# Three stage starts, two mask tables, one tail and one attention's copies put elsewhere in the queues of a fused two-model kernel

## What is computed

```python
def reference(x, mem, positions, ...):
    x = first_block(x, mem, positions, ...)
    return second_block(x, ...)

# first_block, layer i of 2
x = x + dsa_moba_mixer(h, ...)            # i = 0: top-64 keys for 8 heads, block attention for 8 heads
x = x + nsa_mixer(h, ...)                 # i = 1
x = x + memory_cross_attention(rms_norm(x), rms_norm(mem), ...)
x = x + swiglu(rms_norm(x), ffn_w_in, ffn_w_out)

# second_block, layer l of 2
proj = rmsnorm(x) @ w_in                  # gates 4096, conv 512, three attentions 2048
ys = conformer conv, neighbourhood, dilated and sliding-window attention (4 heads each)
mixed = sum(sigmoid(gate_n + b_n) * (ys_n @ w_branch_n))
x = x + mixed @ w_out
x = x + (silu(gate) * up) @ w_down        # gate, up = split(conv3(rmsnorm(x) @ w_up))
```

## Time and profile before

| | us |
|---|---|
| median of 3 runs | 1684.88 (1684.46 to 1686.14) |
| profiled execution, its own time | 1684.49 |
| its span, first to last instruction | 1682.7 |
| PE busy in it | 1626.0 (97%) |
| DVE busy | 1096.4 (65%) |
| ACT busy | 885.1 (53%) |
| POOL busy | 456.2 (27%) |

### The profile page before, as it was taken

How to read it: one execution, slowest core, us unless ns; L and a number is a source line. 1 busy time by engine, 2 the same in 40 slices (tenths; PEclk the granted TensorE clock), 3 DMA queues, 4 the chain that set the end, 5 groups by cost and what they waited for, 6 DMA issues and landing times. The chain is left out here.

```text
span 1682.7 us, 26946 instructions
## 1 busy us (share of the span) xinstructions
PE 1626.0 (97%) x10929; PEld 1465.7 (87%) x10929; DVE 1096.4 (65%) x1546; ACT 885.1 (53%) x1385; POOL 456.2 (27%) x476
## 2 busy tenths in 40 slices
PE   8989899999999999999999999999999999999999
PEld 7857799987887879998888998999888899889997
DVE  6875656545576765655577668677646866867773
ACT  7454554434455555443446746566445674665652
POOL 2500200002341120000237805144213790504430
PEclk9999999999999999999999999999999999999999
DMA  7522466556340236665554434766556444376652
GB/s 275 171 75 91 110 181 195 178 199 207 103 150 26 76 101 169 187 193 185 177 191 151 151 126 131 197 182 192 180 160 211 155 150 129 127 197 178 189 187 75
DMA packets 287068, 265.30 MB, mean 158 GB/s; under 512 B 12257, under 2 KB 247521, under 8 KB 286945
## 3 DMA queue, kind: packets, MB, share of 16 engines
q1 hardware_dynamic: 286944, 263.59, 50.4%
HBM read 262.52 MB, written 1.05 MB: 157 GB/s over the span
## 5 line engine op out<-in xcount | busy, mean ns | idle before, releaser
L144 DVE TENSOR_TENSOR w_lo<-w_raw,w_hi 128x2048 fp32r<-128x2048 f32 (+2 forms) x244 | 568.8, 2334 | 296.7 <-ACT w_hi L143 294.5
L1863 PE MATMUL bank<-h_hi,w_hi 128*128 128x256 f32 x1984 | 566.2, 285 | 11.9 <-issue 4.6
L143 ACT ACTIVATE w_hi<-w_raw 128x2048 fp32r<-128x2048 f32 (+2 forms) x244 | 462.4, 1901 | 207.4 <-PE bank L529 117.4
L1864 PE MATMUL bank<-h_lo,w_hi 128*128 128x256 f32 x1984 | 561.9, 283 | 0.0
L1865 PE MATMUL bank<-h_hi,w_lo 128*128 128x256 f32 x1984 | 561.9, 283 | 0.0
L1863 PEld LDWEIGHTS bank<-h_hi,w_hi 128*128 128x128 f32 x1984 | 380.8, 192 | 16.4 <-issue 10.9
L1864 PEld LDWEIGHTS bank<-h_lo,w_hi 128*128 128x128 f32 x1984 | 381.0, 192 | 0.1
L1865 PEld LDWEIGHTS bank<-h_hi,w_lo 128*128 128x128 f32 x1984 | 380.9, 192 | 0.0
L456 PE MATMUL bank<-w_hi,h_hi 128*128 128x512 f32 (+1 forms) x288 | 113.5, 394 | 5.4 <-DVE w_lo L144 3.4
L2925 POOL TENSOR_TENSOR cffn_hidden<-cffn_conv 128x256 f32<-128x256 f32 x44 | 72.2, 1642 | 164.3 <-ACT cffn_conv L2955 164.3
L457 PE MATMUL bank<-w_lo,h_hi 128*128 128x512 f32 (+1 forms) x288 | 111.9, 389 | 0.0
(11 more groups left out here) (444 smaller groups left out, 2884.0 us busy)
## 6 DMA issues: line engine op xcount, KB each, us to landing
w_raw<-in_w_in SPq DMA_DIRECT2D x48, 1024.0 KB, 5.0
w_raw<-in_ffn_w_in SPq DMA_DIRECT2D x88, 512.0 KB, 5.1
w_raw<-in_w_up SPq DMA_DIRECT2D x88, 512.0 KB, 5.2
w_raw<-in_ffn_w_out SPq DMA_DIRECT2D x22, 1024.0 KB, 4.9
w_raw<-in_w_down SPq DMA_DIRECT2D x22, 1024.0 KB, 4.9
w_raw<-in_nsa_w_in SPq DMA_DIRECT2D x10, 1024.0 KB, 5.1
w_raw<-in_mem_w_kv SPq DMA_DIRECT2D x8, 1024.0 KB, 5.1
w_raw<-in_w_branch SPq DMA_DIRECT2D x8, 1024.0 KB, 5.1
```

Source lines behind the costliest of these rows:

```text
L143: return act.activation(hi, raw, ACT.Copy)
L144: return dve.tensor_tensor(self.lo[:, cut_slot, 0:k * n], raw, hi.bitcast(F32), ALU.subtract)
L1863: pe.matmul(out, h, hi[:, f, :], start=(f == 0), stop=False)
L1864: pe.matmul(out, h, lo[:, f, :], start=False, stop=False)
```

## The change

1. In mix and cffn: ACT rounds chunk 1 ahead of the squares, DVE cuts it ahead of the spread copy; PE turns the row factors in the middle of job 1 (after its first tile) instead of after job 0.
2. In mix: the third part of `make_masks` leaves the projection for attention step 1, the wait for mask step 12 goes to step 3.
3. In the mix tail: chunk `mix_chunks[0] + 2` is cut ahead of the loop, no more after j = 1.
4. In ab: ACT makes the attention's copies (`copier="act"`), each behind its exponentials. The rounding of the memory's last chunk stands ahead of the second memory copy; DVE waits for segment 5's rotation before `mem.dve(0)`; `mem.dve(1)` goes into attention step 1.

```diff
 class Attention.act
+            if i and self.copier == "act":
+                self.copy_turned(act, i - 1)
             if between is not None:
                 between(act, i)
+        if self.copier == "act":
+            self.copy_turned(act, len(self.pairs) - 1)
+
+    def copy_turned(self, e, j):
+        e.wait_ge(self.turned, j + 1)
+        if j >= 2:
+            e.wait_ge(self.out, j - 1)
+        dims = [[S, 2], [1, self.pairs[j]["keys"]]]
+        to, of = free(self.k.turned[:, j % 2, :], dims), free(self.k.bank[6 + j % 2][:, :], dims)
+        if self.copier == "act":
+            e.activation(to, of, ACT.Copy).then_inc(self.copied, 1)
+        else:
+            e.tensor_copy(to, of).then_inc(self.copied, 1)
 block_dsa_moba, scalar
                 mem.act(act, 0)
+                mem.act_next(act, 1)
                 mem.act(act, 1)
-                mem.act_next(act, 1)
 block_dsa_moba, vector
                 project.dve(dve, sums)
+                hn.wait_done(dve, 5)
                 mem.dve(dve, 0)
                 dve.wait_ge(const, 2)
-                mem.dve(dve, 1)
 ...
+                    if i == 1:
+                        mem.dve(dve, 1)
 stationary_job
+        if tile == 0 and middle is not None:
+            middle(pe)
 block_branches and block_conv_ffn, scalar
                 rows.round(act, range(4, KD))
+                w.round_to(act, 1)
                 for t in range(T):
                     rows.square(act, t, 1)
-                w.round_to(act, 1)
                 row_factors.act(act)
 block_branches and block_conv_ffn, vector
                 rows.cut(dve, range(4, KD))
+                w.cut_to(dve, 1)
                 row_factors.dve(dve)
-                w.cut_to(dve, 1)
 block_branches, vector
-                    if j < 3:
+                    if j < 2:
                         make_masks(dve, j)
 ...
                 def step(dve, i):
+                    if i == 1:
+                        make_masks(dve, 2)
+                    if i == 3:
+                        dve.wait_ge(mask_step, 12)
 ...
-                dve.wait_ge(mask_step, 12)
                 att.dve(dve, finish, step, lambda dve, i: cut(dve, AHEAD + i))
 ...
-                w.cut_to(dve, mix_chunks[0] + 1)
+                w.cut_to(dve, mix_chunks[0] + 2)
 ...
-                    if j % 2 == 1:
+                    if j >= 3 and j % 2 == 1:
                         w.cut_to(dve, mix_chunks[0] + j // 2 + 2)
 block_branches, tensor (block_conv_ffn alike, with j == 1)
-                    stationary_job(k, pe, conv_chunks[i], k.bank[6 + i], rows, None, i == 0)
-                    if i == 0:
-                        row_factors.pe(pe)
+                    stationary_job(k, pe, conv_chunks[i], k.bank[6 + i], rows, None, i == 0, row_factors.pe if i else None)
```

More of the change, by code:

```diff
@@ L701, with __init__ @@
 class Attention:
-    def __init__(self, k, name, pairs, place=None):
+    def __init__(self, k, name, pairs, place=None, copier="dve"):
         s = k.sems
-        self.k, self.pairs = k, pairs
+        self.k, self.pairs, self.copier = k, pairs, copier
         self.place = place or (lambda i, u: (4 + i % 2, u * S))
@@ L801, in dve @@
                 between(dve, i)
[L802 to L811, removed]
+            if 1 <= i <= n and self.copier == "dve":
+                self.copy_turned(dve, i - 1)
             if i >= 3 and self.pairs[i - 3]["last"]:
@@ L1163, in block_dsa_moba @@
                   for t in range(T) for h in (0, 2, 4, 6)]
-        att = Attention(k, "att", pairs, lambda i, u: (4 + u, i % 2 * S))
+        att = Attention(k, "att", pairs, lambda i, u: (4 + u, i % 2 * S), copier="act")
         slot = lambda grp: out[:, grp % 2, (512 if grp < 2 else 0):(1024 if grp < 2 else 512)]\
@@ L1847, in block_memory_ffn, with stationary_job @@
         k.close()
-def stationary_job(k, pe, c, bank, features, free_bank, first=False):
+def stationary_job(k, pe, c, bank, features, free_bank, first=False, middle=None):
     w, hi, lo = k.weights, features.hi, features.lo
@@ L2999, in _ @@
                 for j in range(KF):
-                    stationary_job(k, pe, up[j], k.bank[j % 4], rows, (scaled, j - 3) if j >= 4 else None, j == 0)
-                    if j == 0:
-                        row_factors.pe(pe)
+                    stationary_job(k, pe, up[j], k.bank[j % 4], rows, (scaled, j - 3) if j >= 4 else None, j == 0,
+                                   row_factors.pe if j == 1 else None)
                 down.pe(pe, lambda pe, f: pe.wait_ge(hid_lo, f + 1))
```

## The result

The changed kernel took 1690.75 us (median of 14 runs, 1689.17 to 1693.52), the kernel before beside it 1685.49 (14 runs, 1680.53 to 1689.65). The ratio is 1.0034, with a 95% interval of 1.0025 to 1.0042: slower by 4.2 to 7.1 us. The forecast was 1689.1. The profiled execution of after took 1693.52, the longest of its 14, with a span of 1691.8; so its trace shows 9.1 us more than that of before, of which a typical execution has 5.3. What is too much there lies in the clock and in two stretches that the change doesn't touch, as will be seen.

The account below looks back on a forecast made before the run. TensorE, busy 97% of the span, bounds the kernel: its work plus 57 us idle. Terms +3.4 - 3.0 + 8.0 - 1.3 - 1.8 - 2.5 - 1.6 + 3.0 = +4.2 on 1684.9 give 1689.1 us; range 1678.0 to 1693.0.

Parts of the forecast that it names:

- four starts, waits: Mix and conv FFN starts: chunk 2 cut late, PE waits 1.8 us; +0.57 per mix, +1.14 per conv FFN, +3.4 us.
- masks, in front of the attention: Mix projection without the five mask operations: PE's 2.13 us wait shrinks by 1.5 in each of two layers, -3.0 us.
- masks, stall: Mix attention: mask operations in step 1 take turns with POOL's additions, late copy stalls PE 4.0 per layer, +8.0 us.
- tail: Mix tail: chunk 2 cut ahead of the loop, contention goes, end comes 0.63 sooner per layer; -1.3 us in two layers.
- first block, turn: First block: last memory cut held back, POOL's key rotation ends sooner, scores start at 88.3 instead of 90.08, -1.8 us.
- first block, attention waits: First block's attention: waits for DVE's copy go, new ones come at pairs 2 and 8; -2.5 us.
- clock, first block: First block's attention: low clock after the 1.45 us wait at 118.0 goes, -1.6 us.
- clock, mask stalls: Mix attention: each layer's 4.0 us mask stall lowers the clock, 1.5 each, +3.0 us.
- clock, starts: Mix and conv FFN starts: nothing taken for clock falls behind the 1.8 us waits; 4 x 1.7 kept as a bound.
- Rivals 1 and 2: Mix attention step 1: (1) mask block hides, 1678.1, chance 0.25; (2) POOL loses every second turn, 1681.7, chance 0.17.
- the cut in step 1: First block's attention: the cut in DVE's queue at pair 1 brings a new 1.1 us wait at pair 2.
- rival 3: Block starts: clock falls in two to four of the new 1.8 us waits, +3.4 to +6.8, 1692.5 to 1695.9; chance 0.13.

Follow-up runs that it names:

- chunk 2 first: Changed kernel with ScalarE rounding chunk 2 behind the squares, ahead of the row-factor copy, at the four block starts: 1677.89 us against 1684.99 for the kernel before, ratio 0.9957.
- three of the kernels above: Kernel before with part 1 alone (1695.07 us), with part 1 and chunk 2 rounded ahead of the row-factor copy (1683.26), and with part 3 alone (1684.33).
- the starts alone: Kernel before with part 1 alone (second chunks and row factors): 1695.07 us against 1684.84, ratio 1.0056.
- POOL held to the end: Changed kernel with GpSimd's tap addition 5 held until all five mask operations are done: 1681.75 us against 1684.99 for the kernel before, ratio 0.9977.
- POOL held for three operations: Changed kernel with GpSimd's tap addition 5 held until three of five mask operations are done: 1678.48 us against 1686.04 for the kernel before, ratio 0.9965.

## Why the prediction was near

The forecast was +4.2, the medians differ by 5.3. Its two kinds of terms did not fare alike.

| term | forecast | measured, by stretch |
|---|---|---|
| four starts, waits | +3.4 | +3.6 |
| masks, in front of the attention | -3.0 | -3.4 |
| masks, stall | +8.0 | +6.7 |
| tail | -1.3 | -2.3 |
| first block, turn | -1.8 | -1.7 |
| first block, attention waits | -2.5 | -1.7 |
| sum of waits | +2.8 | +1.2 |
| clock, first block | -1.6 | -3.4 |
| clock, mask stalls | +3.0 | +5.1 |
| clock, starts | 0 | +4.7 |
| sum of clock | +1.4 | +6.4 (profiled execution); some +4 (median) |

The profiled execution's 9.1 us are 1.2 of waits, 6.4 of clock, 0.9 on the way to mix0 and 0.6 in the first microseconds; of the last two the forecast has nothing, and they belong to no part of the change.

**Starts.** Right in mechanism and size. The waits were 1.92, 1.80, 1.92 and 1.81 for a forecast of 1.8, and released by L144. Taking away the link (chunk 2 first) took them away.

**Masks.** Right in mechanism: full turns, not none and not half. The term mis-sized is the block: 7.07 us (906.91 to 913.98) for a forecast of 7.5, with turns of 1.10, 0.98, 0.95 and 0.95 behind a first of 0.41. The stall was 3.33 for 4.0: 0.4 of the difference is the shorter block, since each turn is about 1.0 and not 1.1, the rest the room in front of it, some 3.7 us and not 3.5. Rivals 1 and 2 fall with these rows. In front of the attention it was 1.70 instead of 1.5 for each layer. Operations that read PSUM kept their time (the copy's 0.68, the gate product's 0.68 at 913.90). The Trainium skill (GPSIMD Engine Reference, Key points) names DVE operations in a 2-port mode or with two SBUF inputs as those that contend. The trace agrees for the two operations with two SBUF inputs (0.95 and 0.98 us longer) and for the two that read PSUM; for the three with one SBUF input it would have to be the 2-port mode, which no trace names, though they are the faster ones (0.42 against 0.69).

**Tail.** Right in sign, mis-sized by 1.0 us and outside its bounds (-0.4 to -1.6). The forecast moved the steps from j = 3 on 0.63 sooner and let them run as before. The step that failed is the second half: the cut behind j = 3 is itself 0.56 shorter, since its contest with POOL falls out differently. 0.63 + 0.56 = 1.19 is, to 0.02, the 1.17 of the first layer; the second has 1.15.

**First block.** The turn was right to 0.1. The cost of the cut in step 1 was right too (1.1 for 1.05), and the wait at pair 8 (0.85 for 0.9). The waits that I took from laying out the queues, -2.5, were -1.7; the traces' own difference, 1.3, which I set aside, was nearer from the other side. The clock there was sized at half of what it was: 6.8 us at half the speed cost 3.4 us of PE's busy time, that is all of it, since PE had work throughout.

**Clock.** This is where the forecast fell short, and where it met its number partly by luck: waits were overestimated by 1.6, the clock underestimated by some 3, and the two errors took part of each other away. I gave rival 3 (it falls at the starts too) 0.13, because the present waits of 1.23 don't lower it, and took nothing for the starts, having seen that one of 2.13 didn't. That last reason was no reason: the same 2.13 us wait lowers it in other executions, as three of the kernels above show. I had read one execution as a rule. The same trace held a warning that I passed over: of the two memory attentions, each with a wait of 1.96 us, the first has the low clock behind it and the second not:

```profile
613.88 0.66 PE L1527 MATMUL bank<-ident,mf_att 128*128 128x128 f32 x4 [1.96 <-ACT mf_att L1600]
614.00:617.40 3.40, 3.31 (x19) 2.38 (x19) 3.37 (x5) 2.29 (x8) 1.89 (x2) 1.00 0.12 31
```

Over all 14 traces the count is: behind the waits of 1.80 to 1.93 us at the starts 15 low stretches in 20 places, behind those of 2.13 5 in 14, behind the first 1.96 9 in 14, behind the second none in 14, behind a wait of 1.4 in nsa (430.5 in before, low within 2.4 us of it) 12 in 14, behind the mask stall of 3.3 6 in 6. So the length of the wait alone doesn't decide. The Trainium skill (TensorE: Matmul & The Clock Gate, Part 1) has the throttled state as the default that activity releases; that fits a clock that falls behind idle time, and whether 1.8 us is enough, which the prediction left open, the runs answer with: mostly at the starts, not always. The mean granted clock says the same without a trace: 0.9949 over 29 runs of before, 0.9923 over 14 of after. The difference, 0.0026 of 1690, is an estimated 4.4 us, if PE had work throughout; with the waits' +1.2 that is 5.6, for the 5.3 measured.

**Why the parts don't add up.** Alone they measured +10.2, +8.7, -0.5 and -7.0, +11.4 in all, and together +5.3. The intervals are wide (the starts alone +6 to +13 us), but the table shows a place: the starts alone have two low stretches behind the 2.13 us waits (3.0) and a longer one in the first attention (+2.91). In after, part 2 has shortened the one wait to 0.42 and part 4 has taken away the other's cause. The idle stretches add up, the clock behind them doesn't.

## What to carry to other kernels

Before a step is moved, look at what GpSimd does beside its new place: of five VectorE operations of 0.4 to 0.7 us beside back-to-back additions the first took 0.4 us more and the others about 1.0 each, and one step earlier, with GpSimd idle, nothing more. Where a wait moves to a later point, everything queued behind it on that engine moves too; if any of it can go ahead of the wait, put it there. Take a new idle stretch of TensorE near 2 us as one that can bring a low clock, here 1.5 to 1.6 us each time, even where one trace shows the clock unmoved: at the block starts it did so in 15 of 20 places, in the second memory attention in none of 14. The mean clock of many executions tells more than one trace.

## What the runs showed of the hardware that was not expected

The clock falls behind the same wait in one kernel and not in another. The kernel with POOL held to the end and the one with POOL held for three operations are alike at the starts (waits of 1.93 and 1.81 us in the one, 1.90 and 1.81 in the other). In the first the clock was at its lower level behind all four of them, in the second behind one. The windows view, at cffn0, first of the one and then of the other:

```profile
1070.70:1074.10 3.40, 3.40 (x16) 3.40 (x17) 3.40 (x4) 2.92 (x4) 0.00 (x0) 0.50 0.63 176
```

```profile
1070.90:1074.30 3.40, 3.40 (x28) 3.40 (x29) 3.40 (x4) 2.84 (x4) 0.00 (x0) 1.00 0.69 201
```

It isn't only this execution: the mean clock was 0.993 to 0.996 in 12 runs of the first and 0.996 to 0.997 in 6 of the second, and the kernel with the stall of 0.33 is 3.3 us faster by the medians. What decides stays open: the two kernels ran in different comparisons, so the chip isn't separated from the kernel.

Who waits in a contest depends on who was there first. DVE's cut that began at 915.10 in after kept its 2.28 us, and POOL's addition asked for at 915.24 took 3.28 instead of 1.30; the mask operations asked for during an addition waited for its end. With POOL's short operations on 64 columns (0.32 us alone) beside the same five mask operations in before, DVE lost almost nothing (0.42, 0.54, 0.69, 0.43, 0.69), and POOL's grew to between 0.44 and 0.77.
